# A decoder layer step on Trainium2: the decode work rebuilt around four column groups and one PSUM bank

## The chip, the cores and the metric

One NeuronCore of one Trainium2 chip runs the whole program. The metric is the device time of one execution in microseconds. The kernel before takes 1921.58 us (median of 3 runs, 1921.17 to 1921.85).

## The reference

One layer of a hybrid decoder runs on 256 prompt tokens and on 8 decode requests of one token each. All 264 tokens share every weight matrix.

```
z = h @ w_in                                   # h: layer norm of x, 2048 wide
retention:  S' = gamma*S + k v^T ;  o_r = q . S'          # 4 heads, 256x256 state per request
fox:        sc = q.k/sqrt(128) + c_q - c_k ;  p = softmax(sc) ;  o_f = p @ v   # 8 heads of 128
            # c: running sum of log forget values; decode: 1024 past rows in 8 pages of 128, and its own row
o_r = groupnorm(o_r) * gn_g * silu(rg)
mix = (sigmoid(gr) * (o_r @ w_ret_proj) + sigmoid(gf) * (o_f @ w_fox_proj)) @ w_out
x1  = LN(a*h + mix) ;  y = LN(a*x1 + (silu(x1@w1) * (x1@w3)) @ w2 + sigmoid(x1@w_pg) * (p@w_pe))
```

The outputs are y, the new retention states of prompt and requests (8 states of 1 MB), and the new keys, values and log forget rows. What this case is about is the decode part of fox and retention: for each request 8 pages of keys and 8 pages of values (512 KB each) from a paged cache, and one state of 1 MB.

## The kernel before, in words

**The stream of weights.** Every weight matrix goes through the kernel in *chunks*: 4 tiles of 128 rows by 256 columns. SyncE loads a chunk into one of four slots of `raw` (`load`), ScalarE rounds it to `whi` (`split_hi`), VectorE makes the rest `wlo` (`split_lo`), both three chunks ahead of the product (`AHEAD`), and TensorE (`multiply`) makes 24 products of 264 columns with it: hi*hi and hi*lo (L523, L524), then lo*hi (L528). There are 552 chunks (some with 2 tiles). The moving operand (`hT_hi`, `mix_hi`, `x1_hi`, `g_hi`, ...) is tile `kt` at a distance of 1056 bytes per tile. `whi` and `wlo` are plain rings of 4 x 4096 bytes.

**The phases** follow each other on every engine: `phF` (fox inputs, 2 x 24 chunks), `phR` (retention inputs, 2 x 32), `phG` (gates, 4 x 16), `phYR` (16), `phYF`, `phO`, `phP`, then two halves of the FFN (`up` 11 x 8 chunks, `down`), and the last norm. Between the chunks, and in program order with them, each engine does the side work of the phase.

**The decode windows.** A window is 16 chunks and serves the request before in its softmax and values, and the next one in its key scores. The first window (`"first"`) has key scores only, seven are `"middle"` (3 in `phR`, 4 in `phG`), the last (`"last"`, `phYR`) has values only. So each of the 8 requests goes once through these steps; the positions are chunk numbers in the window:

- `KEY_POS` 0, 2, 4, 6, 8, 9, 11, 13: VectorE multiplies a page of keys with the broadcast query and sums it, 8 heads (L1295).
- position 0: VectorE adds the bias into `scd`, TensorE transposes it, 8 pages, to 8 rows by 1024 (`past_scores_T`, L639).
- positions 1 and 2: maximum, Exp and scaling over 8 partitions x 1025 (`s8`; L1303 to L1311 on VectorE, L963 on ScalarE).
- position 4: TensorE brings the probabilities back to 128 partitions, 8 matrix products (`past_probs_T`, L646), VectorE copies them to `probT`.
- `VALUE_POS` 5, 7, 9, 10, 11, 12, 13, 14: a page of values, two products of 8 x 512 (`past_values`, L657), one in the column group at partition 32 and one at 64.
- positions 14 and 15: ScalarE copies the 8 x 512 results (L969), TensorE picks the diagonal of heads, 8 products (`own_values`, L667), VectorE copies to `ofS`.

GpSimd loads the pages into 4 buffers in the order of use (`load_page`), each when the page four places before it has been used.

**The states.** In each of the 4 iterations of `phG` two states are loaded into the one buffer `stateS`, scaled by ScalarE (`state_scale`, L1046), updated by VectorE (`state_new`, L1404), read by TensorE with 8 products of 8 x 256 (`state_out`, L782, column groups 32 and 64, heads one after the other), accumulated into `or8` by VectorE (`state_read`) and stored. The next load waits for that store.

Of the kernel before, what the change touches and what calls it, by code (L numbers as in the profile page):

```python
# [42 lines left out]
KT = 4  # L43
NC = 256
HEADS = 4
HALVES = (32, 64)
# [4 lines left out]
CREDIT = {"lo_made": RING, "multiplied": RING, "acc0_free": 1, "acc1_free": 1, "page_used": HEADS,  # L51
          "of_made": 1, "or_made": 1, "sc_made": 1, "sc_ps": 1, "r_res": 1, "g_lo_made": 1, "pv_ps": 1, "st_ps": 1}
# [22 lines left out]
def shape_constants(SEQ, DEC, PAST, H_R):  # L75
# [19 lines left out]
        "cos": np.cos(ang), "nsin": -np.sin(ang), "psin": np.sin(ang),  # L95
# [6 lines left out]
    return np.concatenate([np.asarray(a, f) for a in parts.values()], 1).astype(f), where, [float(np.exp(x)) for x in log_g]  # L102

# [59 lines left out]
def layer_kernel(nc, a, where, gammas, dims):  # L163
# [10 lines left out]
    with ctx:  # L174
# [20 lines left out]
        whi = place("whi", [P, RING, KT, NC], F32R)  # L195
        wlo = place("wlo", [P, RING, KT, NC], F32R)
# [8 lines left out]
        stateS = place("stateS", [P, H_R, 2, 256], F32)  # L205
        vbc = place("vbc", [P, H_R, 256], F32)
        page = place("page", [P, PAGES, 1024], F32)
        qbc = place("qbc", [P, 1024], F32)
        s8 = place("s8", [8, 1032], F32)
# [8 lines left out]
        pagesum = place("pagesum", [P, HEADS, P], F32)  # L218
        probT = place("probT", [P, NPG, H_F], F32)
# [3 lines left out]
        ofS = place("ofS", [P, H_F, DEC], F32)  # L223
        rqS = place("rqS", [P, H_R, 2, DEC], F32)
        rkS = place("rkS", [P, H_R, 2, DEC], F32)
        sgS = place("sgS", [P, H_R, 2, DEC], F32)
        orS = place("orS", [P, H_R, 2, DEC], F32)
        prodS = place("prodS", [P, DEC, H_F], F32)

        ov8 = place("ov8", [72, 512], F32, at=made["s8"][0])  # L230
        or8 = place("or8", [72, 512], F32, at=after("ov8"))
# [4 lines left out]
        lfn8 = place("lfn8", [8, DEC], F32)  # L236
        snew8 = place("snew8", [8, DEC], F32)
        pnew8 = place("pnew8", [8, DEC], F32)
        pdiag = place("pdiag", [8, H_F, DEC], F32)
# [59 lines left out]
        assert after("ytok8") <= made["orT_hi"][0]  # L299
        g_hi = place("g_hi", [P, HF2, T], F32R, at=after("uT"))  # L300
        g_lo = place("g_lo", [P, HF2, T], F32R, at=after("g_hi"))
# [15 lines left out]
        page_in = [sem(f"page_in{i}") for i in range(PAGES)]  # L317
# [148 lines left out]
        def _(pe):  # L466
# [45 lines left out]
            def multiply(ph, it, j):  # L512
# [13 lines left out]
                for t in range(c.n_kt):  # L526
                    for m in range(2):
                        last = mm(backward(acc[c.acc][:, m, 0:T]), wlo[:, s, t, m * P:(m + 1) * P], backward(xh[:, c.kt0 + t, :]),  # L528
                                  start=False, stop=c.last and t == c.n_kt - 1)
# [1275 lines left out]
```

## Time and profile before

| | us |
|---|---|
| median of 3 runs | 1921.58 |
| the profiled execution | 1920.96 |
| its span | 1919.4 |
| PE busy / PEld busy | 1837.4 / 1729.0 |
| DVE busy / ACT busy | 1050.6 / 794.2 |
| granted TensorE clock, mean | 0.979 |

The span is from the first to the last instruction; the 1.6 us around it are in the time of the execution and not in the span. PE is TensorE's matrix products, PEld its weight loads, DVE VectorE, ACT ScalarE, POOL GpSimd. Records of matrix products overlap, since they are pipelined: what one costs is the distance from its start to the start of the next.

### The profile page before, as it was taken

What the parts mean: (1) busy time and instruction counts of PE and PEld (TensorE: products, weight loads), DVE (VectorE), ACT (ScalarE), POOL (GpSimd) and SP (SyncE); (2) the same over time, 40 slices, a digit from 0 to 9 for tenths busy, and PEclk for the clock granted to TensorE, in tenths of its full rate; (3) what the DMA queues carried; (4) which work ended last, traced back from release to release, by engine and by line L of the source; (5) the groups of instructions that cost most, each with busy time, mean ns of one, the idle gap of its engine ahead of it and who ended that gap; (6) DMA issues with size and microseconds to landing.
All of it is one profiled execution on the core that took longest, in us unless ns stands there. A gap on an engine that the chain in (4) does not pass through costs nothing.

```text
span 1919.4 us, 39296 instructions
## 1 busy us (share of the span) xinstructions
PE 1837.4 (96%) x14288; PEld 1729.0 (90%) x14288; DVE 1050.6 (55%) x2098; ACT 794.2 (41%) x930; POOL 156.0 (8%) x268
## 2 busy tenths in 40 slices
PE   6999999999899999999979999999999999999996
PEld 5989998888777887889969999999999999999995
DVE  6443684765756666447656454444444444444554
ACT  4443433434442443333335445555433344433333
POOL 4341001111112112000000000000000000000000
PEclk9999999999899999999989999999999999999998
DMA  6555777877799899445524565555555655555551
GB/s 208 153 155 167 230 231 234 260 266 233 260 330 329 297 323 352 154 153 185 180 89 148 176 192 181 182 179 175 177 180 180 194 179 183 178 180 171 181 180 46
DMA packets 315952, 386.18 MB, mean 201 GB/s; under 512 B 14232, under 2 KB 290968, under 8 KB 315480
## 3 DMA queue, kind: packets, MB, share of 16 engines
q1 hardware_dynamic: 286832, 287.48, 48.1%
q0 software_dynamic: 28688, 97.51, 14.5%
q8 instruction: 51, 0.84, 0.2%
q14 instruction: 29, 0.24, 0.0%
q10 hardware_dynamic: 352, 0.12, 0.0%
HBM read 371.22 MB, written 13.84 MB: 201 GB/s over the span
## 4 chain that ended last, share of the span: by engine, by line
PE 74%; DVE 3%; DMA 2%; issue 2%; ACT 1%; POOLq 0%; DVEq 0%; ACTq 0%; SPq 0%
PE acc L523 23%; PE acc L524 22%; PE acc L528 22%; PE X L657 2%; DMA page<-in_cache_v 2%; PE X L782 1%; PE X L845 1%; PE X L646 1%; DVE pagesum L1295 1%; PE X L667 0%; PE X L639 0%; DVE uT L1543 0%; ACT uT L1104 0%; DVE wlo L454 0%; DVE x_lo L1552 0%
## 5 line engine op out<-in xcount | busy, mean ns | idle before, releaser
L454 DVE TENSOR_TENSOR wlo<-raw,whi 128x1024 fp32r<-128x1024 f32 (+1 forms) x552 | 659.8, 1204 | 643.4 <-ACT whi L449 636.3
L449 ACT ACTIVATE whi<-raw 128x1024 fp32r<-128x1024 f32 (+1 forms) x552 | 568.8, 1037 | 677.3 <-PE acc L528 668.4
L523 PE MATMUL acc<-x_hi,whi 128*128 128x264 f32 x1664 | 413.2, 285 | 10.4 <-DVE x_lo L1552 6.8
L524 PE MATMUL acc<-x_lo,whi 128*128 128x264 f32 x1664 | 412.5, 284 | 0.0
L523 PE MATMUL acc<-hT_hi,whi 128*128 128x264 f32 x1408 | 367.0, 296 | 1.1 <-POOL hT_lo L1640 1.1
L524 PE MATMUL acc<-hT_lo,whi 128*128 128x264 f32 x1408 | 356.3, 289 | 0.0
L523 PEld LDWEIGHTS acc<-x_hi,whi 128*128 128x128 f32 x1664 | 313.9, 189 | 11.4 <-issue 7.2
L524 PEld LDWEIGHTS acc<-x_lo,whi 128*128 128x128 f32 x1664 | 315.3, 189 | 0.0
L523 PEld LDWEIGHTS acc<-hT_hi,whi 128*128 128x128 f32 x1408 | 271.1, 193 | 44.3 <-issue 38.4
L524 PEld LDWEIGHTS acc<-hT_lo,whi 128*128 128x128 f32 x1408 | 272.2, 193 | 0.1
L528 PE MATMUL acc<-x_hi,wlo 128*128 128x264 f32 x1664 | 236.3, 285 | 0.0
L528 PEld LDWEIGHTS acc<-x_hi,wlo 128*128 128x128 f32 x1664 | 216.2, 189 | 0.0
L528 PE MATMUL acc<-hT_hi,wlo 128*128 128x264 f32 x1408 | 202.1, 287 | 0.0
L528 PEld LDWEIGHTS acc<-hT_hi,wlo 128*128 128x128 f32 x1408 | 185.2, 191 | 0.2 <-DVE wlo L454 0.2
L524 PE MATMUL acc<-g_lo,whi 128*128 128x264 f32 x704 | 175.5, 284 | 0.0
L523 PE MATMUL acc<-g_hi,whi 128*128 128x264 f32 x704 | 175.5, 286 | 0.0
L524 PEld LDWEIGHTS acc<-g_lo,whi 128*128 128x128 f32 x704 | 132.4, 188 | 0.0
L523 PEld LDWEIGHTS acc<-g_hi,whi 128*128 128x128 f32 x704 | 132.3, 188 | 0.0
L1295 DVE CUSTOM_DVE_ANT_0 pagesum<-page,qbc 128x128 f32<-128x128 f32 x512 | 113.6, 285 | 5.9 <-DMA page<-in_cache_k 4.5
L528 PE MATMUL acc<-g_hi,wlo 128*128 128x264 f32 x704 | 101.1, 285 | 0.0
L528 PEld LDWEIGHTS acc<-g_hi,wlo 128*128 128x128 f32 x704 | 91.8, 188 | 0.0
L657 PE MATMUL X<-page,probT 128*8 128x512 f32 x256 | 68.2, 612 | 11.1 <-DMA page<-in_cache_v 11.0
(313 smaller groups left out, 1701.9 us busy)
## 6 DMA issues: line engine op xcount, KB each, us to landing
raw<-in_w SPq DMA_DIRECT2D x256, 512.0 KB, 4.1
raw<-in_w_in SPq DMA_DIRECT2D x176, 512.0 KB, 5.0
page<-in_cache_k POOLq DMA_DIRECT2D x64, 512.0 KB, 5.8
page<-in_cache_v POOLq DMA_DIRECT2D x64, 512.0 KB, 6.0
raw<-in_w_out SPq DMA_DIRECT2D x32, 512.0 KB, 4.5
raw<-in_w_pg SPq DMA_DIRECT2D x32, 512.0 KB, 3.5
stateS<-in_state_ret POOLq DMA_DIRECT2D x8, 1024.0 KB, 7.5
out_ret_state_sample<-stateS POOLq DMA_DIRECT2D x8, 1024.0 KB, 6.8
```

The lines of the kernel that those rows point to most:

```text
L449: nc.scalar.activation(whi[:, s, 0:k, :], raw[:, s, 0:k, :], ACT.Copy).then_inc(S["hi_made"], 1)
L454: nc.vector.tensor_tensor(wlo[:, s, 0:k, :], raw[:, s, 0:k, :], whi[:, s, 0:k, :].bitcast(F32), ALU.subtract).then_inc(S["lo_made"], 1)
L523: mm(backward(acc[c.acc][:, m, 0:T]), w, backward(xh[:, c.kt0 + t, :]), start=c.first and t == 0, stop=False)
L524: mm(backward(acc[c.acc][:, m, 0:T]), w, backward(xl[:, c.kt0 + t, :]), start=False, stop=False)
L528: last = mm(backward(acc[c.acc][:, m, 0:T]), wlo[:, s, t, m * P:(m + 1) * P], backward(xh[:, c.kt0 + t, :]), start=False, stop=c.last and ...
L646: last = mm(X[:, 0, p * 8:p * 8 + 8], s8[:, p * P:(p + 1) * P], ident[0:8, 0:8], start=True, stop=True)
L657: last = mm(X[g:g + H_F, 0, :], probT[:, p, :], page[:, s, half * 512:half * 512 + 512], start=p == 0, stop=p == NPG - 1)
L782: last = mm(X[g:g + DEC, 3, i % 2 * 256:(i % 2 + 1) * 256], rqS[:, i, d, :], stateS[:, i, d, :], start=d == 0, stop=d == 1)
L845: last = mm(X[:, 1, 0:T], const("ones"), lnsq[:, q % 2, k, :], start=q == 0 and k == 0, stop=q == 3 and k == 3)
L1295: V.tensor_tensor_reduce(out=pagesum[:, i % HEADS, :], in0=page[:, s, i * P:(i + 1) * P], in1=qbc[:, i * P:(i + 1) * P], scale=1.0, scalar ...
```

## The change

The two engines that shared the softmax over 8 partitions now keep the scores where they are, at 128 key rows per partition.

- **Softmax in score layout.** VectorE takes the maximum over the pages (`pmax`, 128 x 8), TensorE transposes this one tile (`past_max`, position 0), VectorE reduces it to 8 maxima and puts them on a diagonal, one product with ones spreads them to all partitions (`past_max_spread`, position 1), VectorE subtracts, ScalarE takes Exp of 128 x 64 at position 3, and VectorE sums and multiplies with a one-hot row of the request (`pp`, 128 x 512) at position 4. Nothing is divided there: the request's own key and the sums of all requests are handled once, in `phYR` (`wnew`, `psumS`).
- **Values and states in one bank each.** `past_values` makes 8 products of 8 x 128, two in each of four column groups. Because `pp` has zeros in the columns of the other requests, all requests accumulate in one bank, which `add_zero` opens and closes. `own_values`, `past_scores_T` and `past_probs_T` are gone. `state_out` makes 8 products of 8 x 256, one per head and half, heads in the four groups, in bank 3, with queries `rqz` that are zero in other requests' columns.
- **States.** TensorE reads the state as it is loaded (two buffers); gamma is put into the query, and the new key's term is added at the end from q.k and v. Scaling, update and store of the states move to the first 8 iterations of the first `up` phase, in a buffer of their own (`stateF`, `vbcF`), after a second load.
- **Layout.** The slots of `whi` and `wlo` start at bytes 64, 4288, 8512 and 12736, so 4224 apart; `g_lo` starts at a multiple of 256 bytes behind `g_hi`.
- The key sums are written over the page (`head`) with one semaphore step per page; the rows of retention keys are transposed in two parts (positions 2 and 4 of the second half).

```diff
+SLOT_AT = (16, 1072, 2128, 3184)
+SLOTS_END = 4224
+def slot_of(w, s):
+    return w[:, SLOT_AT[s]:SLOT_AT[s] + KT * NC].rearrange("p (t n) -> p t n", t=KT)
...
+            def add_zero(bank, start):
+                return mm(X[:, bank, 0:256], const("mask")[:, P:2 * P], cst[:, 0:256], start=start, stop=not start)
+            def past_max(slot):
+                pe.wait_ge(S["sx_made"], line(slot, 1, 0))
+                pe.wait_ge(S["pmax_made"], line(slot, 1, 0))
+                tr(X[0:H_F, 1, 0:P], pmax[:, :], ident).then_inc(S["pmaxT_ps"], 1)
+            def past_max_spread(slot):
+                pe.wait_ge(S["pmax8_made"], line(slot, 1, 0))
+                mm(X[:, 1, P:P + H_F], const("ones")[0:8, :], pmax8[:, :], start=True, stop=True).then_inc(S["pmaxS_ps"], 1)
...
-                for half, g in enumerate(HALVES):
-                    last = mm(X[g:g + H_F, 0, :], probT[:, p, :], page[:, s, half * 512:half * 512 + 512],
-                              start=p == 0, stop=p == NPG - 1)
+                for e in range(2):
+                    for q in range(4):
+                        last = mm(X[q * 32:q * 32 + DEC, 0, e * P:(e + 1) * P], pp[:, p, q * 2 + e, :],
+                                  page[:, s, (q * 2 + e) * P:(q * 2 + e + 1) * P], start=False, stop=False)
...
             def state_out(it, n):
-                for i in range(H_R):
-                    g = HALVES[i // 2]
-                    for d in range(2):
-                        last = mm(X[g:g + DEC, 3, i % 2 * 256:(i % 2 + 1) * 256], rqS[:, i, d, :], stateS[:, i, d, :],
-                                  start=d == 0, stop=d == 1)
+                pe.wait_ge(st_in[n], it * 16 + 16)
+                pe.wait_ge(S["rqz_made"], it * 2 + (n + 1))
+                for d in range(2):
+                    for i in range(H_R):
+                        last = mm(X[i * 32:i * 32 + DEC, 3, 0:256], rqz[:, i, d, :], stateS[:, n, i, d, :], start=False, stop=False)
...
+            pe.wait_ge(S["prod_made"], 3)
+            for d in range(2):
+                last = mm(X[:, 2, 0:32], const("ones"), small[:, 2, d * 32:d * 32 + 32], start=d == 0, stop=d == 1)
+            last.then_inc(S["new_ps"], 1)
+            add_zero(3, True)
...
+                if pos == 2:
+                    dve.wait_ge(S["pmaxS_ps"], line(slot, 1, 0))
+                    V.tensor_copy(pmaxS[:, :, batch].rearrange("s h o -> s (h o)"), X[:, 1, P:P + H_F])
+                    V.tensor_tensor(scd[:, :, :], scd[:, :, :], X[:, 1:2, P:P + H_F].broadcast_to([P, NPG, H_F]), ALU.subtract)\
+                        .then_inc(S["sx_made"], 1)
                 if pos == 4:
+                    dve.wait_ge(S["exp_made"], line(slot, 1, 0))
+                    dve.wait_ge(S["pv_ps"], line(slot, NPG, 1 - NPG))
+                    V.tensor_reduce(psumS[:, :, batch].rearrange("s h o -> s (h o)"), by_page, axis=AX.X, op=ALU.add)
...
+                        if states and j == 5:
+                            act.wait_ge(S["fs_in"], it * 16 + 16)
+                            for i in range(H_R):
+                                st = stateF[:, i, :, :].rearrange("p d e -> p (d e)")
+                                last = A(st, st, ACT.Copy, scale=gammas[i])
...
+                        if states and j == 6:
+                            dve.wait_ge(S["fs_scaled"], it + 1)
+                            dve.wait_ge(S["fs_vb"], it * 16 + 16)
+                            for i in range(H_R):
+                                for d in range(2):
+                                    last = V.scalar_tensor_tensor(out=stateF[:, i, d, :], in0=vbcF[:, i, :], scalar=rk1[:, i, d, :],
+                                                                  in1=stateF[:, i, d, :], op0=ALU.mult, op1=ALU.add)
...
+            with pool.Fori(0, DEC) as it:
+                pool.dma_start(stateF[:, :, :, :].rearrange("p h d e -> p (h d) e"),
+                               a["state_ret"][ds(it, 1)].rearrange("o h (d p) e -> p (o h d) e", p=P)).then_inc(S["fs_in"], 16)
+                pool.dma_start(vbcF[:, :, :].rearrange("p h e -> p (h e)"), v_rows[ds(it, 1), :].partition_broadcast(P)).then_inc(S["fs_vb"], 16)
+                pool.wait_ge(S["fs_new"], it + 1)
+                pool.dma_start(a["ret_state_sample"][ds(it, 1)].rearrange("o h (d p) e -> p (o h d) e", p=P),
+                               stateF[:, :, :, :].rearrange("p h d e -> p (h d) e")).then_inc(S["fs_stored"], 16)
+                pool.wait_ge(S["fs_stored"], it * 16 + 16)
```

## Rows read from the trace of the kernel before

**Rows 1.** The page: busy us, share of the span and instructions of each engine.
```profile
PE 1837.4 (96%) x14288; PEld 1729.0 (90%) x14288; DVE 1050.6 (55%) x2098; ACT 794.2 (41%) x930; POOL 156.0 (8%) x268
```

**Rows 2.** The page: the chain that ended last, share of the span by engine.
```profile
PE 74%; DVE 3%; DMA 2%; issue 2%; ACT 1%; POOLq 0%; DVEq 0%; ACTq 0%; SPq 0%
```

**Rows 3.** Timeline of TensorE (start, us): two column groups, one page of values.
```profile
363.96 1.03 PE L657 MATMUL X<-page,probT 128*8 128x512 f32 x4
364.92 0.39 PE L523 MATMUL acc<-hT_hi,whi 128*128 128x264 f32 x1
```

**Rows 4.** Timeline of TensorE: one read of a state, and what follows.
```profile
517.48 2.76 PE L782 MATMUL X<-stateS,rqS 128*8 128x256 f32 x16
520.17 0.39 PE L523 MATMUL acc<-hT_hi,whi 128*128 128x264 f32 x1
```

**Rows 5.** Timeline of TensorE: four column groups in turn (the forget product).
```profile
41.32 1.99 PE L492 MATMUL X<-h,wff 128*32 128x264 f32 x32
43.24 0.39 PE L523 MATMUL acc<-hT_hi,whi 128*128 128x264 f32 x1
```

**Rows 6.** Timeline of TensorE: score transposes, probabilities back, diagonal of heads.
```profile
408.23 1.04 PE L639 MATMUL X<-cst,scd 128*8 128x128 f32 x8
...
357.33 1.95 PE L646 MATMUL X<-cst,s 8*128 8x8 f32 x16
359.21 0.39 PE L523 MATMUL acc<-hT_hi,whi 128*128 128x264 f32 x1
...
403.75 1.52 PE L667 MATMUL X<-cst,ov 8*128 8x1 f32 x16
```

**Rows 7.** Timeline of TensorE: the products of successive chunks (phO, then down).
```profile
930.76 1.13 PE L528 MATMUL acc<-mix_hi,wlo 128*128 128x264 f32 x8
933.65 1.13 PE L528 MATMUL acc<-mix_hi,wlo 128*128 128x264 f32 x8
936.57 1.13 PE L528 MATMUL acc<-mix_hi,wlo 128*128 128x264 f32 x8
...
1380.56 1.14 PE L528 MATMUL acc<-g_hi,wlo 128*128 128x264 f32 x8
1383.49 1.13 PE L528 MATMUL acc<-g_hi,wlo 128*128 128x264 f32 x8
```

**Rows 8.** Waits of TensorE: us in total, times, longest.
```profile
PE X L657 <- DMA page<-in_cache_v: 11.0, 6, 2.7
PE X L639 <- DVE scd L1282: 8.4, 3, 5.8
```

**Rows 9.** Stretches: us, busy PE, PEld, DVE, ACT, POOL; PEclk, DMA share, GB/s.
```profile
344.70:408.20 63.50, 62.11 (x456) 53.44 (x457) 46.64 (x175) 19.34 (x21) 8.99 (x17) 0.97 0.82 274
562.10:633.70 71.60, 68.87 (x489) 56.05 (x490) 46.63 (x177) 27.85 (x34) 13.74 (x23) 0.95 0.94 320
704.50:769.90 65.40, 62.62 (x464) 51.02 (x464) 45.24 (x175) 25.51 (x32) 11.76 (x20) 1.00 0.94 331
1126.00:1149.20 23.20, 23.20 (x194) 23.20 (x193) 11.04 (x10) 12.09 (x12) 0.00 (x0) 1.00 0.57 180
```

**Rows 10.** Stretch behind a L646 of phG, TensorE alone (PEclk third from last).
```profile
575.70:579.70 4.00, 4.00 (x28) 0.78 0.89 297
```

**Rows 11.** Groups by line: VectorE's key sums and state update, ScalarE's state scaling.
```profile
L1295 DVE CUSTOM_DVE_ANT_0 pagesum<-page,qbc 128x128 f32<-128x128 f32 x512 | 113.6, 285 | 5.9 <-DMA page<-in_cache_k 4.5 <-DVE scd L1282 1.1
L1404 DVE SCALAR_TENSOR_TENSOR stateS<-vbc,rk,stateS 128x256 f32<-128x256 f32 x64 | 26.0, 479 | 0.3
L1046 ACT ACTIVATE stateS<-stateS 128x512 f32<-128x512 f32 x32 | 17.5, 616 | 8.0 <-DMA stateS<-in_state_ret 8.0
```

**Rows 12.** The page, DMA issues: KB each, us from issue to landing.
```profile
page<-in_cache_v POOLq DMA_DIRECT2D x64, 512.0 KB, 6.0
stateS<-in_state_ret POOLq DMA_DIRECT2D x8, 1024.0 KB, 7.5
out_ret_state_sample<-stateS POOLq DMA_DIRECT2D x8, 1024.0 KB, 6.8
```

More of the change, by code:

```diff
@@ L299, in layer_kernel @@
         assert after("ytok8") <= made["orT_hi"][0]
+        stateF = place("stateF", [P, H_R, 2, 256], F32, at=made["lnsq"][0])
+        vbcF = place("vbcF", [P, H_R, 256], F32, at=made["ytok"][0])
+        ovS = place("ovS", [P, 256], F32, at=made["qbc"][0])
+        wnew = place("wnew", [P, 4, 64], F32, at=after("ovS"))
         g_hi = place("g_hi", [P, HF2, T], F32R, at=after("uT"))
-        g_lo = place("g_lo", [P, HF2, T], F32R, at=after("g_hi"))
+        g_lo = place("g_lo", [P, HF2, T], F32R, at=(after("g_hi") + 255) // 256 * 256)
         assert after("g_lo") <= made["usum"][0]
@@ L628, in new_scores @@
                 pe.wait_ge(S["f_o_lo"], 2)
-                pe.wait_ge(S["snew_made"], 1)
-                for b in range(DEC):
-                    last = mm(X[0:H_F, 0, b:b + 1], prodS[:, b, :], const("ones")[:, 0:1], start=True, stop=True)
-                last.then_inc(S["snew_ps"], 1)
-            def past_scores_T(slot):
-                pe.wait_ge(S["of_made"], line(slot, 1, 0))
-                pe.wait_ge(S["sc_made"], line(slot, 1, 1))
-                for p in range(NPG):
-                    last = tr(X[0:H_F, 1 + p // 4, (p % 4) * P:(p % 4 + 1) * P], scd[:, p, :], ident)
-                last.then_inc(S["sc_ps"], 1)
@@ L642, in past_probs_T @@
-            def past_probs_T(slot):
-                pe.wait_ge(S["of_made"], line(slot, 1, 0))
-                pe.wait_ge(S["p8_made"], line(slot, 1, 0))
-                for p in range(NPG):
-                    last = mm(X[:, 0, p * 8:p * 8 + 8], s8[:, p * P:(p + 1) * P], ident[0:8, 0:8], start=True, stop=True)
-                last.then_inc(S["p8_ps"], 1)
+                pe.wait_ge(S["prod_made"], 2)
+                mm(X[:, 0, 0:64], const("ones"), prodS[:, :, :].rearrange("p h b -> p (h b)"), start=True, stop=False)
@@ L671, in window @@
+                if sort == "last" and p == NPG - 1:
+                    last = add_zero(0, False)
+                last.then_inc(S["pv_ps"], 1)
             def window(sort, slot, pos):
@@ L1325, in rope @@
+            pick0 = where["pick_b"][0]
             def rope(ph, it, j, dst):
@@ L1602, in _ @@
                                 .then_inc(S["g_lo_made"], 1)
+                n_states = 0 if half else DEC
+                if n_states:
+                    with dve.Fori(0, n_states) as it:
+                        up_step(it, True)
+                with dve.Fori(n_states, up.iters) as it:
+                    up_step(it, False)
                 with dve.Fori(0, down.iters) as it:
```

377 lines of the change are left out of this document (179 added, 198 removed).

## The prediction, made before the changed kernel was run

> **What bounds the kernel now.** I read the page first, then the chain, then stretches by phase, then single bursts of TensorE. TensorE is busy 1837.4 of 1919.4 us and VectorE and ScalarE half of that [rows 1]; the chain that ended last runs 74% over TensorE and no more than 3% over anything else [rows 2]. So what a side step costs is, first of all, its length on TensorE, and work on VectorE or ScalarE counts only where TensorE waits for it. Its waits are few: 11.0 us for pages of values, 8.4 us for `scd`, of which 5.8 us are one wait between `phR` and `phG` [rows 8]. The FFN runs without a gap: 23.20 of 23.20 us, VectorE 11.04 and ScalarE 12.09, DMA share 0.57 [rows 9]. The steady iterations of `phG` are another matter: 71.6 us each at a DMA share of 0.94, 320 GB/s and a granted clock of 0.95 [rows 9]. There the memory is nearly full too, and this is where most of the change acts.
>
> **Part 1, products removed from TensorE, per request.** I take start to start.
>
> - Values: one page takes 0.96 us, four pass records of 512 columns [rows 3]. One after the other, at the pace of a group alone, they would take twice that: the two groups overlap. After, a page has 8 products of 128 columns in two passes, 16 records in four groups. A record of 128 columns in one group has (1.04 - 0.27)/7 = 0.11 us (L639, where 0.27 is the length of the last record) [rows 6]. Four groups in turn do overlap fully: 32 records of 264 columns took 1.92 us, 0.06 us each [rows 5], while the 16 records of 256 columns of a state read, which overlap only where the head changes group, took 2.69 us, 0.17 each [rows 4]; a column costs as much in L639, so 256 of them in one group cost 0.22. 264 columns in four groups at 0.06 make 128 columns 0.029, and 16 of them 0.47 us; with the switch of groups 0.54. Bounds: 0.47, with no switch, and 16 x 0.11 = 1.76 without overlap. I take 0.54, because rows 5 is the same pattern in the same kind of bank: -0.42 x 8 = -3.4 us.
> - State reads: 2.69 us [rows 4] become 16 records of 256 columns in four groups, 16 x 0.06 = 0.96 (bounds 0.93 and 16 x 0.22 = 3.5): -1.7.
> - Score transposes: eight (0.79 = 8 x 0.1) become one: -0.7 [rows 6].
> - Probabilities back: 1.88 [rows 6] goes; the spread of maxima is one product in two records, 2 x 0.12 from the same row: -1.6.
> - Diagonal of heads: 1.52 less 0.07 overhang [rows 6], and one switch in and out: -1.5.
>
> Together 8.9 us, times 8 requests: **-71**.
>
> **Part 2, the layout.** Chunks come in two lengths: starts at 930.76, 933.65 and 936.57 are 2.89 and 2.92 us apart, and in `down` 2.93 [rows 7]; over all undisturbed chunks even slots have 2.917 and odd ones 2.890, in `down` 2.917 and 2.924. Slots are 4096 bytes apart, so their place modulo 256 is always the same, while tile `kt` of the moving operand moves on by 1056 (32 modulo 256): even chunks have moving tiles 0, 32, 64, 96 bytes off, odd ones 128 to 224. The slow products are those of tiles 2 and 3 of even chunks. The new slots shift by 128 modulo 256 from one to the next and follow the moving operand, with a distance of +64 to -32 in every chunk, which is within the fast distances of before; `g_lo` is brought into line with `g_hi`. If that is the cause, 228 even chunks gain 0.027 and 88 chunks of `down` 0.03: -8.8. If the cause is another, the odd chunks may become slow too: +6 to +9. I take **-6**.
>
> **Part 3, what is added or becomes late.**
>
> - Position 0 and 1: TensorE now asks for `pmax` behind the first chunk and for the diagonal behind the second; before it had the diagonal products of L667 in between and nothing at position 1. VectorE reaches them behind a split of 1.2 us, and at position 1 also behind a page of keys (113.6/64 = 1.8 us [rows 11]) in its queue. Lower bound nothing; upper, what rows 8 shows in an ordinary window, 1.3 us twice. I take 0.4 us per request and 1.5 more for each of the two windows that begin in the middle of `phR`, where a rope step stands in the queue: +6. Behind the waiting product, TensorE's whole stream of chunks stands.
> - Pages: in `phG` TensorE waits up to 2.7 us for one page (11.0 us in six waits [rows 8]). That page is loaded when VectorE has finished the key page four places before and lands 6.0 us later [rows 12]; VectorE's pace is not changed, but TensorE comes 2 x 0.42 us earlier. About 0.5 per window, so +3.6 (0 to 6) over seven windows.
> - Between `phR` and `phG` the new product q.k waits for VectorE's last retention step, and now the first chunk stands behind it, where before it ran during the wait of 5.8 us [rows 8]. The chunk (2.9 us, at 1.2 GHz up to 5.8) is partly moved behind the wait: +2.5 (0 to 5). Between `phG` and `phYR` one copy and its hand-overs are added, +1; four zero products of 256 columns, +1.8.
> - VectorE loses `s8` and the state update and gains small steps; it was 46.6 of 63.5 us busy in a `phR` window [rows 9] and will be about 44 of 57. Hidden, but the cover is thin; this is why I charge the waits above.
> - FFN: per state ScalarE 4 x 0.616 = 2.5 us, VectorE 8 x 0.479 = 3.8 us [rows 11], DMA 1 MB in, 1 MB out and 0.5 MB of v. Per iteration that makes ScalarE 14.6 and VectorE 14.9 of 23.2 us [rows 9], and the splits run three chunks (8.7 us) ahead. The states go through one buffer in a chain: load 7.5, scale 2.5, update 3.8, store 6.8 [rows 11, 12], and 1.8 for two issues, 22.4 us against 23.2. Those landing times are from the crowded `phG`; at a share of 0.57 plus this traffic (2.6 MB in 23.2 us, 113 GB/s on 180) they should be shorter. Hidden: 0. Without cover, each us over costs 8.
>
> Sum of part 3: **+15**.
>
> **Part 4, the clock.** A steady `phG` iteration has a granted clock of 0.95, the last one 1.00 [rows 9]: 0.05 x 71.6 = 3.6 us, in two falls. One of them lies behind L646, whose products have 8 rows and 8 columns (a clock of 0.78 in 4 us there, so partly at 1.2 instead of 2.4 GHz [rows 10]), the other behind the late page. The first should go, four times 1.8 us; others may come behind the new waits. I take **-3** (0 to -8).
>
> **Sum.** -71 - 6 + 15 - 3 = -65. The profiled execution took 1920.96 us (span 1919.4 and 1.6 around it), 0.6 below the median. 1921 - 65 = **1856 us**. A steady `phG` iteration should come to about 60 us.
>
> **A rule that speaks against part 1.** Rows 6 shows eight transposes with a new weight each at 0.11 us apart, though all use all rows, and by rows 1 the loads are busy 1729.0 us beside 1837.4 us of products. The Trainium skill, "TensorE: Matmul & The Clock Gate", section "Part 3: Packing small matmuls — row/col tiling", says that a weight load overlaps a running product only when its row group differs; here no row group differs. By that rule each of the rounds would show its load. The trace disagrees so far; its result is the third rival below.
>
> **The rivals.**
>
> 1. *Memory becomes the bound of `phG`.* An iteration moves 71.6 us x 320 GB/s = 22.9 MB [rows 9]; two stores and two v rows leave it, 3.1 MB, so 19.8 MB. At 331 GB/s (share 0.94) this is 60 us, just what I expect of TensorE. If both limits don't interleave as well as now and iterations take 65, it is 4 x 5 = 20 us more: 1876. For it: the share of 0.94 twice. Against: in the last iteration the wait was smallest at the highest rate. Chance 0.16.
> 2. *The state chain in the FFN.* If load and store take 1.5 times rows 12, the chain is 22.4 + 7.2 = 29.6 us against 23.2: 8 x 6.4 = 51 less the lead of about 9: 1898. The issue order on GpSimd's queue has nothing else in it, the DMA has room: 0.03.
> 3. *Loads exposed.* One load is 1729/14288 = 0.12 us at most in the mean [rows 1]; four rounds show it per page and per state read, 0.48 x 72 = +35: 1891. Chance 0.03.
> 4. *The four groups don't overlap in one bank* (slower than before). A page then takes 1.76 us in place of 0.96, +51 over 64 pages, a state read 3.5 in place of 2.69, +6; the other removals stay at 3.8 x 8 = -30, the layout -6, part 3 +15, clock -3: 1921 + 33 = 1954. It decides from 1.5 us per page on. Against it: rows 5, the same bank with four groups. Chance 0.02.
> 5. *Better than forecast*: waits of part 3 near nothing and the clock falls gone, 1921 - 71 - 9 + 5 - 8 = 1838. Chance 0.16.
>
> The forecast (1842 to 1870) has 0.60. The range takes in cases 1 and 5 and the bounds of layout (+9), waits and clock: 1834 to 1884. A change of under 0.2% (4 us) can't be told from none here; faster 0.96, same 0.01, slower 0.03.
>
> **What would show it.** Right: the 16 records of a page within 0.6 us, those of a state read within 1.0; no record between the windows' chunks but one transpose, one spread product, pages and states; a `phG` iteration at 58 to 62 us and a DMA share still at 0.93 or more; all chunks of `down` at 2.89 us; the FFN iterations with states 23.1 to 23.2 us long like those without. Wrong: page bursts of 0.8 us or more (loads exposed), an iteration of `phG` above 64 us with waits for pages (memory), chunks still in two lengths (layout), waits of TensorE for whi in the first `up` (state chain), or clock falls as many as now.

## The result, and the profile after

The kernel after takes 1877.85 us (median of 4 runs, 1875.24 to 1879.57) against 1921.38 us of the kernel before in the same session: a ratio of 0.978, 95% interval 0.976 to 0.980. The profiled execution took 1879.57 us, its span 1878.0: 41.4 us less than the one of before, where 65 were forecast.

First the page, in the form of [rows 1] and [rows 2]: busy us, share of the span and instructions of each engine, then the chain that ended last.

```profile
PE 1769.4 (94%) x14755; PEld 1713.2 (91%) x14755; DVE 1024.0 (55%) x2082; ACT 767.8 (41%) x903; POOL 163.1 (9%) x276
...
PE 72%; DVE 8%; issue 7%; DMA 6%; ACT 4%; POOLq 2%; POOL 1%; ACTq 0%; DVEq 0%; SPq 0%
```

TensorE's busy time fell by 68.0 us, about what the removed products were to bring, and the span by 41.4. The chain hints at where the rest went: VectorE, DMA and ScalarE have 18% of it now, 6% before (the shares of before add up to 82% only, so this is no more than a hint). The waits below show it: TensorE has come nearer to things that were hidden behind its work.

From the distance of the chunks' starts I take each phase's length, before and after: `phR` 271.9 and 269.9 us, `phG` 295.5 and 253.1, `phYR` 64.7 and 57.7, the first `up` of the FFN 255.5 and 268.7, everything else within 2 us. The FFN's first loop lost 13.2 us. The split between `phR` and `phG` is in part one of where the line is drawn: before, the wait between them (5.8 us) came behind the first gate chunk, and now (7.4 us) it comes ahead of it, so it moved from `phG` to `phR`. From the first score product of a window to that of the next (L639 before, L642 after) the three retention windows take 221.4 and 215.0 us, and the four gate windows 291.3 and 252.8. So the gate windows gave about what was forecast, and the retention windows 6.4 us, much less than their removed products.

**The bursts.** The timeline of TensorE (start, us), a page of values and what follows, then the last page of a window with the state read behind it; they answer to [rows 3] and [rows 4].

```profile
361.13 0.62 PE L657 MATMUL X<-page,pp 128*8 128x128 f32 x16 [0.25 <-DVE pp L1312]
361.68 0.39 PE L531 MATMUL acc<-hT_hi,whi 128*128 128x264 f32 x1
...
594.81 1.05 PE L771 MATMUL X<-stateS,rqz 128*8 128x256 f32 x16
595.79 0.39 PE L531 MATMUL acc<-hT_hi,whi 128*128 128x264 f32 x1
```

A page takes 0.55 us from start to start (0.96 before) and a state read 0.98 (2.69 before). The four groups overlap in one bank, and no weight load stands in the open.

**The chunks.** The timeline of TensorE, the last eight products of successive chunks in `phO` and in the first `down`, as [rows 7].

```profile
901.83 1.13 PE L536 MATMUL acc<-mix_hi,wlo 128*128 128x264 f32 x8
904.73 1.13 PE L536 MATMUL acc<-mix_hi,wlo 128*128 128x264 f32 x8
907.62 1.13 PE L536 MATMUL acc<-mix_hi,wlo 128*128 128x264 f32 x8
...
1354.53 1.13 PE L536 MATMUL acc<-g_hi,wlo 128*128 128x264 f32 x8
1357.42 1.13 PE L536 MATMUL acc<-g_hi,wlo 128*128 128x264 f32 x8
```

All are 2.90 us apart now. Even chunks gained 0.02 us, odd ones lost 0.007, those of `down` gained 0.024.

**TensorE's waits**, us in total, times, longest, in the form of [rows 8]:

```profile
PE X L642 <- DVE pmax L1284: 12.7, 6, 4.7
PE acc L531 <- ACT whi L457: 11.7, 6, 2.7
PE X L657 <- DMA page<-in_cache_v: 9.9, 6, 2.3
...
PE X L778 <- DVE small L1399: 7.4, 1, 7.4
...
PE X L657 <- DVE pp L1312: 4.5, 5, 1.1
...
PE X L646 <- DVE pmax L1302: 2.1, 1, 2.1
```

The new maximum (`pmax`, 12.7 us) takes the place of `scd` (8.4 us before). The q·k product (L778) has a wait of 7.4 us, the masked probabilities (`pp`) 4.5. For `whi` it waits 11.7 us, before 2.4. The wait for pages, 11.0 before, is 9.9.

**Stretches**: us, busy PE, PEld, DVE, ACT, POOL; PEclk, DMA share, GB/s. Two windows of the gate phase, and two stretches of the first `up`, the first of them undisturbed. They answer to the second to fourth line of [rows 9].

```profile
544.20:603.90 59.70, 55.15 (x547) 50.83 (x548) 35.12 (x155) 21.60 (x23) 10.84 (x19) 1.00 0.92 323
603.90:665.40 61.50, 56.71 (x548) 52.43 (x548) 35.20 (x155) 21.61 (x23) 10.82 (x19) 0.97 0.92 313
...
1098.00:1121.00 23.00, 23.00 (x193) 23.00 (x192) 12.94 (x18) 13.12 (x17) 1.53 (x3) 1.00 0.82 272
1146.00:1171.00 25.00, 22.51 (x185) 22.09 (x183) 12.89 (x19) 12.41 (x15) 2.33 (x3) 1.00 0.77 257
```

Gate windows take about 60 us, as forecast, at a DMA share of 0.92, a little under the 0.93 that was named. In the first `up` the share is 0.77 to 0.82 where it was 0.57, and TensorE has gaps.

**Two places in detail.** The first is the end of the first retention iteration, in the timelines of TensorE, ScalarE and VectorE.

```profile
323.51 1.99 PE L727 MATMUL X<-sqR,cst 128*128 128x256 f32 x8
...
325.54 0.69 ACT L1027 ACTIVATE sqR<-X,cst 128x512 f32<-128x512 f32 x1 [2.07 <-PE X L727]
...
330.05 3.35 DVE L1381 RECIPROCAL sqR<-sqR 128x512 f32<-128x512 f32 x1
...
334.57 1.22 DVE L1383 TENSOR_TENSOR oR<-oR,sqR 128x1024 f32<-128x1024 f32 x1
...
342.61 0.22 DVE L1280 TENSOR_TENSOR scd<-sc,bias_past 128x64 f32<-128x64 f32 x1
...
343.28 0.37 PE L642 MATMUL X<-cst,pmax 128*8 128x128 f32 x1 [4.71 <-DVE pmax L1284]
```

The same two ends in the trace of before:

```profile
325.27 2.00 PE L735 MATMUL X<-sqR,cst 128*128 128x256 f32 x8
...
344.38 0.21 DVE L1282 TENSOR_TENSOR scd<-sc,bias_past 128x64 f32<-128x64 f32 x1
```

From the variance product (L727, starting at 323.5) to the new scores at 342.6 it is 19.1 us, and it was 19.1 before too (325.3 to 344.4). Nothing in this tail became shorter, so TensorE only reaches its end earlier: there it waited 1.9 us before and waits 4.7 now. The second iteration ends in the same way, with 7.4 us against 5.8.

The second place is the fourth state in the first `up`: GpSimd's transfers, then ScalarE, VectorE and TensorE.

```profile
1140.52 0.91 POOL L1770 DMA_DIRECT2D out_ret_state_sample<-stateF  x1 [18.06 <-DVE stateF L1614]
1147.39 0.88 POOL L1765 DMA_DIRECT2D stateF<-in_state_ret  x1 [5.96 <-DMA out_ret_state_sample<-stateF]
...
1166.93 0.90 POOL L1770 DMA_DIRECT2D out_ret_state_sample<-stateF  x1 [18.11 <-DVE stateF L1614]
...
1157.69 1.06 ACT L457 ACTIVATE whi<-raw 128x1024 fp32r<-128x1024 f32 x1 [6.47 <-DMA raw<-in_w]
1158.66 2.17 ACT L1120 ACTIVATE stateF<-stateF 128x512 f32<-128x512 f32 x4
...
1162.96 3.25 DVE L1614 SCALAR_TENSOR_TENSOR stateF<-vbcF,rk,stateF 128x256 f32<-128x256 f32 x8
...
1171.21 0.59 PE L531 MATMUL acc<-x_hi,whi 128*128 128x264 f32 x1 [2.58 <-ACT whi L457]
```

From store to store it is 26.4 us here, where 22.4 were forecast and an iteration has 23.2; the seven distances between the eight stores are 24.9 to 26.4. The 26.4 are made of the store with the issue of the next load 6.9, the load 8.6 (landed at 1156.03), a wait of 2.6, scaling 2.2, a wait of 2.1, the update 3.3 and 0.7 to the next store. Without the two waits it would be 21.7. ScalarE waits 6.5 us for raw weights while the state's load runs, and the state has already landed when those weights come; only behind their split can ScalarE scale, and VectorE updates behind a split of its own. TensorE's iterations there are 23.2 us three times, then 24.6 to 27.9 us five times.

### The profile page after: what moved, and what is told of

The parts are those of the page before. It is cut to its first block, busy times and chain, and to the rows that moved or that the text cites. A ratio compares the mean times of both kernels' runs of the same rounds, so it can differ in the third digit from the quotient of the medians.

```text
span 1878.0 us, 39915 instructions
## 1 busy us (share of the span) xinstructions
PE 1769.4 (94%) x14755; PEld 1713.2 (91%) x14755; DVE 1024.0 (55%) x2082; ACT 767.8 (41%) x903; POOL 163.1 (9%) x276
## 4 chain that ended last, share of the span: by engine, by line
PE 72%; DVE 8%; issue 7%; DMA 6%; ACT 4%; POOLq 2%; POOL 1%; ACTq 0%; DVEq 0%; SPq 0%
PE acc L531 22%; PE acc L532 22%; PE acc L536 22%; DMA raw<-in_w 2%; DVE wlo L462 2%; DMA page<-in_cache_v 2%; POOLq L1674 2%; ACT whi L457 2%; PE X L657 2%; DVE page L1294 1%; PE X L838 1%; DVE stateF L1614 1%; ACT stateF L1120 0%; ACT L457 0%; DVE uT L1555 0%
## 5 line engine op out<-in xcount | busy, mean ns | idle before, releaser
L531 PE MATMUL acc<-x_hi,whi 128*128 128x264 f32 x1664 | 416.0, 287 | 19.8 <-ACT whi L457 11.7
L531 PEld LDWEIGHTS acc<-hT_hi,whi 128*128 128x128 f32 x1408 | 273.2, 194 | 15.7 <-issue 11.7
L1294 DVE CUSTOM_DVE_ANT_0 page<-page,qbc 128x128 f32<-128x128 f32 x512 | 113.6, 286 | 3.9 <-DMA page<-in_cache_k 3.6
L531 PE MATMUL acc<-mix_hi,whi 128*128 128x264 f32 x256 | 63.1, 284 | 0.0
```

The costliest lines, as they stand in the source:

```text
L531: mm(backward(acc[c.acc][:, m, 0:T]), w, backward(xh[:, c.kt0 + t, :]), start=c.first and t == 0, stop=False)
L1294: last = V.tensor_tensor_reduce(out=head, in0=head, in1=qbc[:, i * P:(i + 1) * P], scale=1.0, scalar=0.0, op0=ALU.mult, op1=ALU.add, accum ...
```

## The experiments

Each was timed against the kernel before on the same chip. Ratios are to it, with their 95% interval; the kernel after stands at 0.978 (0.976 to 0.980).

### No states in the FFN (e1)

```
- n_states = 0 if half else DEC
+ n_states = 0        # and no transfers of states
```

> This kernel leaves out the update of the eight states in the first FFN half (no loads, no scaling, no update, no stores; ret_state_sample stays unwritten). In the trace of the kernel after, the eleven iterations of that half's first loop take 268.7 us instead of the 255.5 us before, and the iterations without a state 23.17 us. Theory (the state updates lengthen that loop, whatever the way): all eleven iterations at 23.17 us, 254.9 us in all, so 13 to 14 us less than the kernel after: 1864 us. Rival (the loop is longer for another reason, such as the new address of g_lo): the loop stays near 268 us and the total near 1877 us.

Measured: 1864.25 us, ratio 0.973 (0.971 to 0.975). The eleven iterations of the first `up` take 254.9 us, 23.2 each. So the state updates cost 13.8 us there, and nothing else made that loop longer.

### Transfers of the states alone (e2)

```
- n_states = 0 if half else DEC
+ n_states = 0        # ScalarE and VectorE: no scaling, no update
...
- pool.wait_ge(S["fs_new"], it + 1)
+ pool.wait_ge(S["fs_in"], it * 16 + 16)
+ pool.wait_ge(S["fs_vb"], it * 16 + 16)
+ pool.wait_ge(S["g_made"], it + 1)   # end of the iteration
```

> Keeps the three transfers of each state in the first FFN half (load of the state, load of the value row, store), the store released by the end of the iteration, and leaves out the scaling on ScalarE and the update on VectorE (ret_state_sample gets the old states). Theory A (one buffer: load 9, scaling 2.2, waits 2 and update 3.3, store 6 us run one after the other, 25.7 us against an iteration of 23.2, and the engines wait for the load with the weights' splits behind them): no engine waits for a state, so iterations at 23.2 us, total near 1864 us, as without states. Theory B (the 1 MB transfers delay the weights' own loads, which land after 7.5 to 7.8 us instead of 4.6): most of the 13 us stays, total 1872 to 1878 us, with waits of ScalarE for the raw weights.

Measured: 1865.03 us, ratio 0.972 (0.970 to 0.974). The stretch of the first `up` (columns as above) and ScalarE's waits in it:

```profile
1055.00:1315.00 260.00, 260.00 (x2156) 260.00 (x2155) 124.27 (x113) 134.75 (x135) 17.27 (x22) 1.00 0.79 258
```

```profile
ACT whi L457 <- DMA raw<-in_w: 9.8, 4, 3.9
```

The same bytes run beside the loop, at a share of 0.79, and ScalarE does wait for raw weights, up to 3.9 us. TensorE is busy 260.00 of 260.00 us nevertheless. Theory B alone falls.

### Arithmetic of the states alone (e3)

```
- act.wait_ge(S["fs_in"], it * 16 + 16)
+ act.wait_ge(S["fs_in"], 16)          # one state, loaded once
+ act.wait_ge(S["fs_new"], it + 1)
...
- with pool.Fori(0, DEC) as it:        # GpSimd: one load and one store, no loop
```

> Keeps the scaling (4 on ScalarE, 2.2 us) and the update (8 on VectorE, 3.3 us) in each of the eight iterations but on one state that is loaded once and stored once, so no transfer of a state runs beside the loop (ret_state_sample gets one row only). Theory A (the serial chain through one buffer) and theory B (transfers against weight loads) both give iterations at 23.2 us, total near 1864 us. Theory C (2.2 us on ScalarE and 3.3 us on VectorE ahead of the splits of the weights is what TensorE waits for): the waits for whi stay, 1870 to 1878 us.

Measured: 1865.2 us, ratio 0.973 (0.970 to 0.975); the same stretch:

```profile
1055.00:1315.00 260.00, 260.00 (x2156) 260.00 (x2155) 148.74 (x187) 142.81 (x160) 0.91 (x1) 1.00 0.60 188
```

VectorE has 24.5 us more in it than in e2, ScalarE 8.1, and TensorE again no gap. Theory C falls too. Neither the transfers nor the arithmetic cost anything alone; the 13.8 us exist only where both run in the same iterations.

### A state in every second iteration (e4)

```
- with act.Fori(0, n_states) as it:
-     up_step(it, True)
+ with act.Fori(0, pairs) as i2:
+     up_step(i2 * 2, True, i2 + first)   # 5 pairs in the first half, 3 in the second
+     up_step(i2 * 2 + 1, False)
```

> All the work of the kernel after, but a state only in every second iteration of the first loop, of both FFN halves: five in the first, three in the second. Theory A (chain of 25.7 us against an iteration of 23.2): a chain has 46.4 us now, nothing waits for it, both halves' first loops near 255 us, total near 1864 us. Theory B (transfers delay the weights): the same eight sets of transfers lie beside the same loads, so the loss of 13 us stays for the most part, spread over both halves: 1872 to 1878 us. Theory C: as B.

Measured: 1864.77 us, ratio 0.972 (0.970 to 0.974), the whole computation. TensorE in the first `up` is without a gap, at a DMA share of 0.72. With 46.4 us for a chain that takes 26.4, the loss is gone, though every transfer and every instruction is still there. That is what theory A demands.

It doesn't single theory A out, though. B and C at once, weights that land late and arithmetic in the queues ahead of their splits, with no one waiting for the buffer, would also be harmless in every second iteration. ScalarE's waits in the kernel after, 1060 to 1340 us, speak for that as much as for the buffer:

```profile
ACT whi L457 <- DMA raw<-in_w: 30.1, 14, 6.5
ACT stateF L1120 <- DMA stateF<-in_state_ret: 9.5, 3, 3.9
```

In three of the eight iterations the scaling waits for its state; in four it stands right behind a split that waited for late weights. A kernel with a second buffer for the state would tell the two apart; it was not run.

### The q·k product earlier (e5)

```
+ if it and j == 25:
+     dve.wait_ge(S["rvS_made"], 4)
+     V.tensor_tensor(small[:, 2, :]..., rqS, rkS, ALU.mult)   # moved from behind ret_result_lo(1, 1)
```

> VectorE's product of the retention query and key rows is issued in the second retention iteration at chunk 25 instead of behind the last results of that iteration. In the kernel after, TensorE waits 7.4 us for that product ahead of the first gate chunk, and runs that chunk (5.0 us) at the low clock. Theory (the step sits in TensorE's path): the wait goes, TensorE starts the gate phase at once, 5 to 8 us less, 1867 to 1873 us. Rival (the tail of the last retention iteration, from the variance product to the new scores 19.1 us, sets the start of the next window, so the wait only moves to the window's first product): 0 to 2 us less.

Measured: 1876.72 us, ratio 0.978 (0.975 to 0.980), no change. TensorE's waits in the kernel after from 320 to 480 us, and then in this one:

```profile
PE X L642 <- DVE pmax L1284: 5.8, 2, 4.7
```

```profile
PE X L642 <- DVE pmax L1284: 13.6, 3, 7.8
```

The wait of 7.4 us for `small` (in the list above) is gone and one of 7.8 for the next window's maximum stands at the end of the first gate chunk. In this trace the last retention window is 8.4 us shorter and the first gate window 8.9 longer. The rival was right: the product was not the cause, the tail of VectorE and ScalarE was.

### A copy in place of the reciprocal, after and before (e6, e7)

```
- link.step(V.reciprocal(sqR[:, :, 1, :], sqR[:, :, 0, :]))
+ link.step(V.tensor_copy(sqR[:, :, 1, :], sqR[:, :, 0, :]))
```

> Leaves the division out of the retention normalization: VectorE copies the root (2 x 256 columns) instead of taking its reciprocal (3.35 us each in the trace of the kernel after, twice); the outputs of the retention change. Theory R (the normalization's chain, 19.1 us from the variance product to the new scores, and no longer TensorE's own work, sets the length of each retention iteration after the change): 2 x 2.7 = up to 5.4 us less, 1872 to 1874 us. Rival (TensorE's work or the pages set it): no more than 1 us less.

> The same edit in the kernel before: the reciprocal in the retention normalization becomes a copy. Theory R: before the change TensorE has more work of its own in this stretch and its waits there are shorter, so the kernel before gains less than the kernel after, 0 to 3 us of 1921. If it gains the same 5.4 us, the chain set the end in both kernels, and the forecast's 18 us for this phase were never to be had.

Measured: in the kernel after 1870.39 us, ratio 0.975 (0.973 to 0.978); in the kernel before 1918.04 us, ratio 0.999 (0.998 to 1.0004). TensorE's waits of the first, 320 to 480 us:

```profile
PE X L778 <- DVE small L1399: 4.5, 1, 4.5
...
PE X L642 <- DVE pmax L1284: 2.9, 2, 1.8
```

Each of the two waits became 2.9 us shorter (4.7 to 1.8, 7.4 to 4.5), as the copy is shorter than the reciprocal. That is shown in the trace. The totals point the same way, about 6 us less for the kernel after and 2 for the one before, but the intervals touch those of no change or nearly so. The waits of the kernel before with the copy, 300 to 500 us:

```profile
PE X L639 <- DVE scd L1282: 4.0, 1, 4.0
```

It had two waits there, 1.9 and 5.8 us; one is gone and the other is 4.0, 3.6 us less together, against 5.8 in the kernel after. So in the traces, one execution each, the kernel before gains less; by the times it is not shown.

### exp(-0.5 ln) in place of root and reciprocal (e8)

```
- A(sqR[:, :, 0, :], X[:, 2, :]..., ACT.Sqrt, bias=eps_gn, scale=1.0 / 256.0).then_inc(S["r_std"], 1)
+ link.step(A(sqR[:, :, 0, :], X[:, 2, :]..., ACT.Ln, bias=eps_gn, scale=1.0 / 256.0))
+ A(sqR[:, :, 1, :], sqR[:, :, 0, :], ACT.Exp, scale=-0.5).then_inc(S["r_std"], 1)
```

> The whole computation, with another way to the inverse root in the retention normalization: ScalarE takes exp(-0.5 ln(v/256 + eps)) from the sums of squares, and VectorE's reciprocal (3.35 us, twice) goes. Theory R (the tail of each retention iteration, 19.1 us from the variance product to the new scores, sets when the next window can begin): it becomes 19.1 - 3.35 + 0.6 (second function) + at most 1.3 (second table load) = 16.5 us, so up to 2.7 us less in each of the two iterations, and about what the kernel with a copy in the reciprocal's place gave (ratio 0.975 to the kernel before against 0.978): 1868 to 1873 us. Rival (the two table loads on ScalarE delay its splits by as much): no difference to the kernel after.

Measured: 1873.76 us, ratio 0.978 (0.975 to 0.980): no difference that can be told. The timeline of ScalarE:

```profile
324.70 0.69 ACT L1027 ACTIVATE sqR<-X,cst 128x512 f32<-128x512 f32 x1 [2.07 <-PE X L727]
325.40 1.28 ACT L1028 ACT_TABLE_LOAD   x1
326.70 0.63 ACT L1028 ACTIVATE sqR<-sqR 128x512 f32<-128x512 f32 x1
```

The second function has a table load of its own, 1.28 us. The Trainium skill, "ScalarE: Activation LUTs", section "What ACT_TABLE_LOAD costs", puts the load at 1283 ns, as here, and a drain of 1380 ns beside it; here the load starts 0.01 us after the function ahead of it ends and the next function 0.02 us behind it, so the trace shows no drain. TensorE's wait in the first iteration fell from 4.7 to 3.3 us, half of what the copy brought.

### The old addresses (e9)

```
- SLOT_AT = (16, 1072, 2128, 3184)
+ SLOT_AT = (0, 1024, 2048, 3072)
- g_lo = place(..., at=(after("g_hi") + 255) // 256 * 256)
+ g_lo = place(..., at=after("g_hi"))
```

> The kernel after with the old addresses of the split weights (four slots without gaps from 0) and of g_lo (right behind g_hi). In the trace of before the 24 records of a chunk take 2.890 us in odd slots, 2.917 in even ones, 2.92 in the down products; in the kernel after 2.897 in all. Theory (the address alone makes this): chunks return to 2.890 / 2.917 / 2.92 us, and the total gets longer by about 0.5 x 460 x 0.020 - 0.5 x 460 x 0.007 + 88 x 0.024 = 5 us, 1881 to 1884 us. Rival (the shorter cadence comes from something else in the change): no difference.

Measured: 1883.95 us, ratio 0.982 (0.980 to 0.984). The timeline of TensorE in `phO`:

```profile
902.90 1.13 PE L536 MATMUL acc<-mix_hi,wlo 128*128 128x264 f32 x8
905.81 1.13 PE L536 MATMUL acc<-mix_hi,wlo 128*128 128x264 f32 x8
908.71 1.13 PE L536 MATMUL acc<-mix_hi,wlo 128*128 128x264 f32 x8
```

The medians over all chunks are 2.917 in even slots, 2.890 in odd ones and 2.917 to 2.924 in `down`, the lengths of the kernel before to the nanosecond. So addresses alone make them. Which property of the addresses does it is not shown: the slots and `g_lo` moved together, and no other places were tried. By the chunks the layout is worth 5.1 us, by the ratios 8, with an interval that holds 5.

### Maximum one chunk later (e11)

```
  if pos == 1:
-     past_max_spread(slot)
+     (past_max_spread if slot[0] is None else past_max)(slot)   # the spread at pos == 2
```

> In the gate phase alone, TensorE takes the transposed maximum at chunk 1 of a window instead of chunk 0, and the spread of the maximum at chunk 2 instead of 1; VectorE's two steps behind them move with them. The kernel after has TensorE waiting at chunk 0 of each window for the maximum, 12.7 us in six waits, for ScalarE's gate function (0.6 us and a table load of 1.3) is ahead of its two splits. Theory P (the gate phase is bound by TensorE's path): the waits go and 8 to 12 us with them, 1866 to 1870 us. Rival M (the phase is bound by the pages: the DMA share is 0.91 there): the waits for pages grow by as much, within 2 us of the kernel after.

Measured: 1881.2 us, ratio 0.981 (0.978 to 0.983), slower if anything. TensorE's waits in its gate phase:

```profile
PE X L646 <- DVE pmax L1305: 8.6, 4, 2.3
PE X L657 <- DMA page<-in_cache_v: 8.0, 4, 2.4
```

This tells nothing of the memory. The wait for the maximum went, and one of the same size came a chunk later for its spread, because VectorE has a page of keys in front of it at that position. Waits for pages are 8.0 us (7.6 in the kernel after), so they did not grow as the rival would have it. The edit moved the wait and did not remove it.

### Small state loads (e12)

```
- pool.dma_start(stateS[:, n, :, :, :]..., a["state_ret"][ds(k, 1)]...)
+ pool.dma_start(stateS[:, n, 0, 0:1, :], a["state_ret"][ds(k, 1), 0, 0:P, :]...)
```

> In the gate phase each state's load of 1 MB becomes one of 128 KB, and TensorE's eight products per request read that one block (the states' part of the sample output is wrong; all instructions of the engines stay). That takes 0.9 of some 17 MB from each window. Rival M of the prediction (the gate phase is bound by the memory: 61 us windows at a DMA share of 0.91): windows shorter by up to 3 us each, 6 to 12 us less in all, 1866 to 1872 us. Theory P (TensorE's own work and its waits for the new maximum and the scores set it): no more than 2 us less, 1876 us.

Measured: 1872.41 us, ratio 0.977 (0.975 to 0.979). TensorE's waits in the gate phase:

```profile
PE X L642 <- DVE pmax L1284: 6.2, 3, 2.1
PE X L657 <- DVE pp L1312: 4.2, 4, 1.1
PE X L657 <- DMA page<-in_cache_v: 2.9, 4, 2.0
```

Waits for pages fall from 7.6 to 2.9 us in the phase, those for VectorE stay as they are. Each window holds the loads of two states, so what goes is 1.8 MB of some 19 per window, and not the 0.9 MB of the expectation. At the 320 GB/s of these windows 1.8 MB are 5.7 us (an estimate). In its trace the gate phase is 7.7 us shorter, 1.9 per window, which holds fewer falls of the clock too; by the ratios it is 3 us, within the intervals. Between the two theories: the memory is a part of the windows' length, 1 to 2 us each, and not their bound.

### The three edits that keep the computation, together (e10)

```
+ # e4 (states), e5 (q·k product) and e8 (exp of ln) in one kernel
```

> The whole computation with three edits to the kernel after: a state only in every second iteration of the first loop of both FFN halves (alone 0.9722 of the kernel before, against 0.978), the product of query and key rows at chunk 25 of the last retention iteration (alone no gain: its wait came back as a wait for the first maximum), and exp(-0.5 ln) instead of root and reciprocal (alone 0.9776). Theory (the retention tail is what early product and shorter tail share, so together they give what the product alone could not: 2.7 to 4 us; the states' 11 to 13 us are apart from it): 0.970, 1860 us against 1918. Rival (only the states' part shows): 0.972, 1865 us.

Measured: 1860.87 us, ratio 0.971 (0.969 to 0.973), the best of all kernels here, 14 us below the kernel after by the ratios, 17 by the medians. The states' part alone gives 0.972, so the other two add 3 us by the ratios and 4 by the medians, with intervals that overlap: this measurement doesn't separate them from nothing. TensorE still waits 6.4 us for the first maximum of the gate phase.

## Why the prediction was right or wrong

The time lies in the range (1834 to 1884), 22 us above the forecast, and the direction was right. It lies outside the 1842 to 1870 that had 0.60, next to the 1876 of rival 1, whose mechanism is not what happened: that the range held is in part luck, since its upper end was there for other reasons. Point by point, in the forecast's own terms:

- **Part 1, products removed (-71).** Right in mechanism and size: 0.55 us per page against 0.54, 0.98 per state read against 0.96. Start to start, the five groups of products take 120.9 us in the trace of before and 45.9 in that of after, so -75, a few of them at the lower clock. The cadence of a forget product in four groups [rows 5] was the right row for it. Rivals 3 and 4 fall with that. The Trainium skill, "TensorE: Matmul & The Clock Gate", section "Part 3: Packing small matmuls — row/col tiling", lets a weight load overlap a running product only where its row group differs; all these use all rows, and the 16 loads of a page (0.09 us each) don't show in its 0.55 us. The measurement decides against the rule as it is put there.
- **Part 2, layout (-6).** Right in size; -5.1 by the chunks, shown by e9. Odd chunks got 0.007 us slower, where the part left them as they were. That the distance modulo 256 bytes is the reason was an assumption and stays one.
- **Part 3, waits in the decode part (+13 of the +15, the rest being the zero products).** Too low by 5. By the list of waits the maximum has 12.7 + 2.1 where `scd` had 8.4, the q·k product 7.4, `pp` 4.5, L692 0.9, and pages 1.1 less: +18. (The 0.9 us at L692 are the scores' step in the middle of `phR`.) The step that was mis-sized is the one between `phR` and `phG` and its twin in the middle of `phR`. I charged +2.5 for a new product and 1.5 for a rope step, and took for granted that removed products shorten a retention window. Both iterations end with a tail on VectorE and ScalarE that the change doesn't touch, 19.1 us in the first, so 2.8 and 1.6 us of TensorE's gain went into waiting. e5 (the wait comes back elsewhere) and e6 (both waits shrink by the shorter operation) show it. The zero products took 3.4 us and not 1.8. A wait of 5.8 us for `scd` [rows 8] was in my rows; I read it as a wait to be added to and not as the end of a chain.
- **Waits for the maximum in the steady windows** (2.1 us each) come from ScalarE: gate function 0.61, table load 1.28 and two splits 2.0 stand ahead of VectorE's split, and the scores behind it. I charged 0.4. The pages, where I put +3.6, gave -1.1.
- **FFN states (0, "hidden").** Wrong, +13.8 us, and the largest miss. e1 gives the size, e2 and e3 show that each half is hidden alone, and e4 that both together cost nothing when every second iteration is free of them. The forecast had the chain, 22.4 against 23.2 us, and rival 2 beside it at 0.03. The term that failed is one it put at nothing without a reason: the waits inside the chain, 4.8 us in the iteration shown. Scaling and update stand in queues at fixed chunks, behind splits that themselves wait for weights delayed by the state's load. The transfers as a whole were not mis-sized: the forecast said they "should be shorter", the store was (5.9 us against 6.8), the load was not (8.6 against 7.5), and with the issues both make 15.5 us against 16.1. So rival 2's condition, 1.5 times the landing times, did not occur. The lead of the splits hid the excess for three iterations and not for the other five. Whether TensorE pays for the buffer's chain or for late weights and arithmetic in one queue stays open (see e4).
- **Part 4, the clock (-3).** The gain did not come. From `phR` to the fall right behind `phYR` TensorE has 47.8 us at the lower clock against 44.4 before, so about +2; the mean granted clock of the two profiled executions is 0.976 and 0.979. One fall more in one execution each is no proof of the sign, but fewer falls there are not. Those behind the probabilities' products (at 506, 578 and 650 us before) went, as forecast, and new ones stand at waits for the maximum (at 273, 342, 604 and 666 us; none at the one of 544 us) and at that for `small` (471 us). Stretches of TensorE in the kernel after, PEclk third from last: behind the wait of 2.1 us at 603.9, behind 7.4 and behind 4.7:

```profile
604.70:608.70 4.00, 4.00 (x23) 0.60 1.05 340
475.80:482.40 6.60, 6.57 (x32) 0.56 0.64 200
343.30:347.30 4.00, 4.00 (x19) 0.50 0.50 140
```

  A granted clock of 0.50 is 1.2 GHz. So a wait that is followed by 3.4 us at the lower clock costs about 1.7 us beside its own length, half of that stretch (an estimate).
- **Rival 1, memory as the bound of `phG`.** Not so at 60 us: e12 takes 1.8 MB from each window, 5.7 us at 320 GB/s, and the windows get 1 to 2 us shorter. The remark against it, that the wait was smallest at the highest rate, misreads the trace of before: the last iteration's longest wait for a page was 2.3 us and the third's 2.0.

In sum, with the measured terms (products, layout, waits, zero products, clock, states): -75 - 5 + 18 + 3 + 2 + 14 = -43, where the trace has -41.4. With the forecast's -71 and 2 for the products and zero products it is -40.

What stays open: which of the two explanations holds for the loss in the FFN (no kernel with two state buffers was run), what it is in the addresses that changes the chunks, how much time the kernel before would gain from a shorter retention tail (e7's interval ends just past no change), and how far memory alone would hold a gate window once the waits for the maximum are gone, since e11 moved them and didn't remove them.

## What to carry to other kernels

When the busiest engine gets shorter, list first the places where it already waits, and follow what it waits for back to its last release by that same engine: a chain of 19 us on the others that begins with a product and ends in front of one doesn't shrink with the work in between. Transfers that are hidden alone and arithmetic that is hidden alone need not be hidden together. Cost the whole load, compute, store chain with landing times at the DMA share it creates itself and with the waits at its place in each queue, and look for a length well below the period; giving it every second period was free here. When a wait is taken away, look in the trace for where it comes back before the next edit.

## What the runs showed of the hardware

- Sixteen records of 128 columns that go round four column groups take 0.034 us each, with weights of 128x8 of their own each time; the loads (0.09 us each in the trace) stay hidden, though none of them differs in its row group.
- The addresses of the weights and of the moving operand change 24 records of 264 columns by about 1%: 2.890, 2.917 or 2.924 us with the old ones, 2.897 in all chunks with the new ones (e9).
- VectorE's reciprocal of 128x512 takes 3.35 us, where the product of 128x1024 takes 1.22.
- A function of the logarithm and one of the exponential right behind it each had a table load, 1.28 us.
- Transfers of 1 MB from GpSimd's queue beside a stream of 512 KB loads: the loads land after 6.9 us (median of ten, 1120 to 1148 us), against 4.0 in the same stretch of the kernel before.
